# Rotary embedding applied head by head in the attention units, the first tile's blocks solved on VectorE, the third tile prepared with the first two

## What is computed

```python
qd, kd, vd = split(silu(short_conv(concat([qb, kb, vb]))))
qd, kd = l2_norm(qd per head), l2_norm(kd per head)
qd, kd = apply_rope(qd, cos, sin), apply_rope(kd, cos, sin)     # latent tokens only
# apply_rope, per pair: out = (x1*c - x2*s, x1*s + x2*c)
# per chunk: a = strict_lower((k*beta) @ k.T * decay); t_inv = inverse(eye + a)
# scan over chunks: v_new = t_inv-corrected values; o = q @ S + intra @ v_new; S = S*decay + k.T @ v_new
```

## Time and profile before

| | us |
|---|---|
| median of three runs | 1311.85 (1308.52 to 1314.66) |
| the profiled execution | 1310.18 |
| its span, first to last instruction | 1308.3 |
| attention units, about | 170 to 412 |
| delta phase: preparation | 412 to 473 |
| delta phase: loop over pairs | 473 to 634 |

### The profile page before, as it was taken

How to read it: one execution, slowest core, us unless ns; L and a number is a source line. 1 busy time by engine, 2 the same in 40 slices (tenths; PEclk the granted TensorE clock), 3 DMA queues, 4 the chain that set the end, 5 groups by cost and what they waited for, 6 DMA issues and landing times.

```text
span 1308.3 us, 15852 instructions
## 1 busy us (share of the span) xinstructions
PE 1148.9 (88%) x6262; PEld 615.6 (47%) x6262; DVE 435.0 (33%) x784; ACT 327.0 (25%) x585; POOL 194.8 (15%) x330
## 2 busy tenths in 40 slices
PE   2699999999989759589999999999839999999990
PEld 1244456666655458589544444444423333333330
DVE  1233036666655714355530200123341111111115
ACT  4021134544543323232321000011201111111111
POOL 0000020011000377474100000000110111111100
PEclk9799999999989869799999999999859999999995
DMA  7801241435110011310211111131615999999936
GB/s 319 353 16 58 96 167 67 162 112 193 65 65 31 19 25 24 101 23 5 93 69 60 65 64 65 65 145 80 241 39 181 393 380 369 385 384 385 382 126 245
DMA packets 44064, 199.98 MB, mean 153 GB/s; under 512 B 18321, under 2 KB 23905, under 8 KB 31953
## 3 DMA queue, kind: packets, MB, share of 16 engines
q1 hardware_dynamic: 28256, 142.03, 28.3%
q10 hardware_dynamic: 4608, 30.18, 6.2%
q0 software_dynamic: 11120, 26.70, 5.6%
HBM read 190.69 MB, written 22.87 MB: 163 GB/s over the span
## 4 chain that ended last, share of the span: by engine, by line
PE 78%; DMA 7%; DVE 5%; POOL 4%; issue 3%; ACT 2%; SPq 0%; POOLq 0%; DVEq 0%; ACTq 0%
PE bank L1599 24%; PE bank L2138 11%; PE bank L1704 9%; PE bank L2159 6%; DMA arena<-h_scratch,arena 3%; PE bank L1753 3%; PE bank L1995 3%; PE bank L1993 3%; PE bank L1690 2%; PE bank L2126 2%; PE bank L1856 2%; PE bank L1661 2%; PE bank L1557 2%; POOL arena L628 1%; DMA arena<-in_w_blocks 1%
## 5 line engine op out<-in xcount | busy, mean ns | idle before, releaser
L1599 PE MATMUL bank<-arena 128*128 128x512 f32 x720 | 316.0, 595 | 4.4 <-DVE arena L1094 3.5
L1599 PEld LDWEIGHTS bank<-arena 128*128 128x128 f32 x720 | 135.3, 190 | 169.5 <-issue 168.4
L2138 PE MATMUL bank<-arena 128*32 128x512 f32 x1536 | 172.9, 601 | 1.3 <-DVE arena L1512 1.3
L1704 PE MATMUL bank<-arena 128*128 128x320 f32 x384 | 121.9, 451 | 0.0
L2138 PEld LDWEIGHTS bank<-arena 128*32 128x32 f32 x1536 | 48.3, 110 | 108.4 <-issue 108.4
L2159 PE MATMUL bank<-arena 128*32 128x512 f32 x768 | 87.4, 595 | 0.8 <-ACT arena L1034 0.8
L1704 PEld LDWEIGHTS bank<-arena 128*128 128x128 f32 x384 | 68.5, 193 | 25.6 <-issue 2.0
L1525 DVE TENSOR_TENSOR arena<-arena,bank 128x256 f32<-128x256 f32 x24 | 10.1, 421 | 176.3 <-ACT arena L1028 176.3
L692 POOL DMA_INDIRECT y_scratch<-arena x24 | 24.4, 1015 | 248.2 <-DVE arena L1518 248.2
L1390 DVE TENSOR_TENSOR arena<-arena,bank 128x512 f32<-128x512 f32 x10 | 6.9, 687 | 135.8 <-PE bank L1995 135.8
L957 ACT ACTIVATE arena<-bank 128x512 f32<-128x512 f32 x20 | 11.9, 597 | 151.5 <-PE bank L1599 151.5
(11 more groups left out here) (292 smaller groups left out, 1522.8 us busy)
## 6 DMA issues: line engine op xcount, KB each, us to landing
arena<-in_w_up SPq DMA_DIRECT2D x32, 2048.0 KB, 15.4
arena<-in_w_blocks SPq DMA_DIRECT2D x27, 2048.0 KB
arena<-in_w_down ACTq DMA_DIRECT2D x28, 1024.0 KB, 8.9
arena<-y_scratch SPq DMA_DIRECT2D x10, 512.0 KB, 10.6
arena<-in_bias POOLq DMA_DIRECT2D x3, 1536.0 KB, 12.1
arena<-in_w_down SPq DMA_DIRECT2D x4, 1024.0 KB, 8.1
arena<-in_x SPq DMA_DIRECT2D x5, 512.0 KB, 9.6
gram_scratch<-arena SPq DMA_DIRECT2D x10, 256.0 KB, 2.5
```

The source lines that it names most:

```text
L1599: last = mm(bank, hT[:, k, tok0[i]:tok0[i] + P], w[:, k, :], start=(k == 0), stop=(k == KC - 1))
L1704: last = mm(banks[5 + half][:, 0:HTOK], w[:, k, :], hT[:, k, half * HTOK:(half + 1) * HTOK], start=(k == 0), stop=(k == KC - 1))
L2138: last = mm(banks[2 + e % 2][at, :], rowsT[e % 2][:, k, at], eup[expert % SLOTS_W][:, k, :], start=(k == 0), stop=(k == KC - 1))
```

## The change

- **Rotation.** The four rotated tiles of the preparation become `scaled(i)`: one instruction each. The rotation moves into the attention units, a head at a time for all four latent tiles (128 x 256 elements an instruction), in three parts of two instructions, in the units that are 11, 12 and 13 behind the chunk's start. Its sines and cosines are loaded by POOL during the attention (into the buffer of the context values), and ACT's square of the next head waits for the last part (`rope_done`), since the temporary shares the square's buffer.
- **First solve.** Pair 0's blocks are solved by DVE (`first_solve`: a copy, then 15 steps of a product and a negated sum along the row), in buffers of its own, and spread by DVE (`first_spread`). POOL makes the third mask of pair 0 at once and starts with pair 1's solve; its spread and solve of later pairs keep their form.
- **Third tile.** Pair 2's `row_sums`, `decay_exp`, `decay_pre`, `key_key`, `gram_out` and pair 1's `key_query`, `intra_out` are done in the preparation, so pass 0 of the loop has only its three levels. POOL solves pair 2 in pass 1, around the third mask.
- **SP.** The scratch traffic of pairs 0 to 2 stands ahead of the wait for the z gate, in a new order; `solved_out(0)` waits for DVE's `intra_out(1)`, which is behind `first_solve` on DVE.

The core of the diff:

```diff
@@ SP, in the queue ahead of gb0
-                if turn:
-                    sp.wait_ge(*read_by(IN_SLOT[slot][turn - 1]))
                 if name == "gb0":
                     gram_out(0)
                     blocks_in(0)
+                    gram_out(1)
+                    blocks_in(1)
                     solved_out(0)
-                    gram_out(1)
                     solved_back(0)
-                    for p in (1, 2):
-                        blocks_in(p)
-                        solved_out(p)
-                        solved_back(p)
-                        gram_out(p + 1)
+                    gram_out(2)
+                    solved_out(1)
+                    solved_back(1)
+                    blocks_in(2)
+                    solved_out(2)
+                    solved_back(2)
+                    gram_out(3)
+                if turn:
+                    sp.wait_ge(*read_by(IN_SLOT[slot][turn - 1]))
@@ POOL, attention
+                if m == 2:
+                    pool.wait_ge(S["pv_mm"], 8)
+                    pool.wait_ge(S["k_out"], 32)
+                    pool.dma_start(rope, t["rope"]...).then_inc(S["b_in"], 16)
@@ POOL, delta phase
             masks(0, 1)
             masks(0, 2)
-            solve(0, 0, SUB - 1)
-            spread_out(0)
+            masks(0, 3)
             for p in range(T):
                 if p == 0:
-                    solve(1, 0, 6)
-                    masks(0, 3)
-                    solve(1, 6, SUB - 1)
-                    q_scaled(1)
-                    masks(1, 1)
-                    pool.wait_ge(S["rope_done"], T)
-                    spread_out(1)
-                    masks(1, 2)
+                    solve(1, 0, SUB - 1)
+                elif p == 1:
+                    solve(2, 0, 6)
+                    masks(1, 3)
+                    solve(2, 6, SUB - 1)
                 else:
                     masks(p, 3)
-                    ...
+                if p + 1 < T:
+                    q_scaled(p + 1)
+                if 2 <= p < T - 1:
+                    solve(p + 1, 0, SUB - 1)
+                if p + 1 < T:
+                    masks(p + 1, 1)
+                    spread_out(p + 1)
+                    masks(p + 1, 2)
@@ ACT
             def head_squared(c):
                 act.wait_ge(S["tok_ready"], c + 1)
                 if c >= 1:
-                    act.wait_ge(S["sqsum"], c)
+                    act.wait_ge(S["rope_done"], c)
...
             kq_out(0)
             decay_exp(0)
+            kq_out(1)
+            kq_out(2)
             z_out(2)
-            kq_out(1)
+            decay_exp(1)
             z_out(3)
-            kq_out(2)
-            decay_exp(1)
-            z_out(4)
             kq_out(3)
             kq_out(4)
+            decay_exp(2)
+            z_out(4)
...
-                if p + 2 < T:
+                if 1 <= p < T - 2:
                     decay_exp(p + 2)
@@ DVE, attention
+            def rotated(c, part):
+                pairs = qkv[:, 1:T, c * P:(c + 1) * P].rearrange("p t (c two) -> p t c two", two=2)
+                x1, x2_ = pairs[:, :, :, 0], pairs[:, :, :, 1]
+                cos, sin = rope[:, :, 0, :], rope[:, :, 1, :]
+                if part == 0:
+                    dve.wait_ge(S["b_in"], 16)
+                    step(v.tensor_tensor(ropet[:, 0], x1, sin, ALU.mult))
+                    step(v.tensor_tensor(ropet[:, 1], x2_, sin, ALU.mult))
+                if part == 1:
+                    step(v.tensor_tensor(x1, x1, cos, ALU.mult))
+                    step(v.tensor_tensor(x2_, x2_, cos, ALU.mult))
+                if part == 2:
+                    step(v.tensor_tensor(x1, x1, ropet[:, 1], ALU.subtract))
+                    step(v.tensor_tensor(x2_, x2_, ropet[:, 0], ALU.add), "rope_done")
...
+                for part in range(3):
+                    if conv_chunk(u, 11 + part) is not None and conv_chunk(u, 11 + part) < 2 * H_B:
+                        rotated(conv_chunk(u, 11 + part), part)
@@ DVE, delta phase
+            def first_solve():
+                dve.wait_ge(S["first_io"], 32)
+                step(v.tensor_copy(first_g[0:32], first_raw[0:32].rearrange("p k i -> p i k")))
+                for i in range(1, SUB):
+                    part = first_t[0:64, 0:i * i].rearrange("p (c k) -> p c k", c=i)
+                    step(v.tensor_tensor(part, first_x[0:64, 0:i, 0:i], first_g[0:64, i, 0:i].unsqueeze(1).to_broadcast([64, i, i]), ALU.mult))
+                    step(v.tensor_reduce(first_x[0:64, 0:i, i:i + 1], part, AX_X, ALU.add, negate=True))
...
-            rotated(0)
+            scaled(0)
             decay_pre(0)
+            scaled(1)
             tok_out(11, 3, 2)
-            dve.wait_ge(S["b_in"], 32)
-            rotated(1)
+            scaled(4)
             gram_out(0)
-            rotated(4)
             intra_out(0)
+            x_flat = first_x[0:64].rearrange("p c i -> p (c i)")
+            step(v.memset(x_flat, 0.0))
+            step(v.memset(x_flat[:, 0:SUB * SUB:SUB + 1], 1.0))
             decay_pre(1)
-            rotated(2)
+            scaled(2)
+            scaled(3)
             gram_out(1)
-            rotated(3)
+            first_solve()
+            intra_out(1)
             dve.wait_ge(S["kqT_ready"], 2 * T)
-            dve.wait_ge(S["gexp_done"], 1)
+            decay_pre(2)
+            first_spread()
+            gram_out(2)
@@ PE, delta phase
             kq_turn(0)
             key_key(0)
-            z_block(2)
             kq_turn(1)
+            kq_turn(2)
+            z_mm(2, 0)
             key_query(0)
+            z_mm(2, 1)
+            row_sums(1)
             z_block(3)
-            kq_turn(2)
-            row_sums(1)
-            z_block(4)
             key_key(1)
             kq_turn(3)
             kq_turn(4)
             pe.wait_ge(S["kqT_ready"], 2 * T)
+            key_query(1)
+            z_mm(4, 0)
+            row_sums(2)
+            z_mm(4, 1)
+            key_key(2)
             turn_inv(0, 1)
```

More of the change, by code:

```diff
@@ L228, in build @@
         solve_t = ring[:, 0, solve_at + SUB * SUB:solve_at + 2 * SUB * SUB]
+        first = [unit[d]["xs"].rearrange("p h c -> p (h c)") for d in range(2)]
+        first_g, first_x, first_raw = (v.rearrange("p (a b) -> p a b", a=SUB) for v in
+                                       (first[0][:, 0:SUB * SUB], first[0][:, SUB * SUB:], first[1][:, 0:SUB * SUB]))
+        first_t = first[1][:, SUB * SUB:]
+        first_in = first_t[:, 0:2 * H_B * SUB].rearrange("p (u i) -> p u i", u=2 * H_B)
         solved_in = solve_t[:, 0:2 * H_B * SUB].rearrange("p (u i) -> p u i", u=2 * H_B)
@@ L414, in erow_of, with mask_of @@
             return unit[d]["erow"][(p - 1) % 3]
+        def mask_of(p, n, d):
+            return unit[d]["cstate"] if (p, n) == (0, 3) else unit[d]["mask"][(NL * p + n) % 2]
         def solve_at_io(p, k):
-            return 48 * p + {"blocks": 32, "solved": 48}[k]
+            return 48 * (p - 1) + {"blocks": 32, "solved": 48}[k]
         def step_at(p, k):
@@ L596, in masks @@
                     pool.wait_ge(S[f"prep{d}"], dprep_at(p, "gram"))
-                    if NL * p + n > 2:
+                    if p >= 1:
                         pool.wait_ge(S[f"x_mm{d}"], NL * p + n - 2)
-                    step(pool.tensor_tensor(U["mask"][(NL * p + n) % 2], U["gramT"][p % 2],
+                    step(pool.tensor_tensor(mask_of(p, n, d), U["gramT"][p % 2],
                                             level_mask[:, d, n - 1, :].unsqueeze(1).to_broadcast([P, H_B, P]), ALU.mult), f"msk{d}")
             def spread_out(p):
-                pool.wait_ge(S["solve_back"], 16 * (p + 1))
+                pool.wait_ge(S["solve_back"], 16 * p)
                 for d in range(2):
@@ L751, in _ @@
             act.wait_ge(S["kctxT_mm"], 1)
-            step(sc.activation(kctxT, banks[6][:, :].rearrange("p (a b) -> p a b", a=4), ACT.Copy), "kctxT_ready")
+            step(sc.activation(kctxT, banks[6][:, :].rearrange("p (a b) -> p a b", a=4), ACT.Copy))
             for u in range(2 * T):
@@ L825, in gate_decays @@
                 step(sc.activation(gt[:, 4:6, :], gt[:, 10:12, :], ACT.Exp))
-                step(sc.activation(gt[:, 9, :], gt[:, 9, :], ACT.Exp), "gexp_done")
+                step(sc.activation(gt[:, 9, :], gt[:, 9, :], ACT.Exp))
             def head_squared(c):
@@ L1838, in turn_inv @@
                     if n == 1:
[L1839 removed]
+                        if p:
+                            pe.wait_ge(S["spread"], 2 * p + d - 1)
+                        else:
+                            pe.wait_ge(S[f"prep{d}"], dprep_at(2, "gram"))
                         if d == 1:
@@ L1855, in couple @@
                     for h in range(H_B):
-                        last = mm(banks[2 * d][:, h * P:(h + 1) * P], U["mask"][(NL * p + n) % 2][:, h], U["inv"][:, h], start=True, stop=True)
```

(1 more changed line is left out.)

81 lines of the change are left out of this document (37 added, 44 removed).

## The result

The changed kernel takes 1290.68 us, median of four runs (1286.11 to 1291.0), against 1311.41 (1308.52 to 1314.66) of four runs of the kernel before: a ratio of 0.9833 with a 95% interval of 0.9806 to 0.986. That is 20.7 us faster, where 17.0 were forecast (1293, range 1286 to 1303).

What follows compares the result with a forecast made beforehand. PE bounds the attention units; in the delta phase PE waits, for SP's late send and POOL's late state store. Gains 9.0 + 9.4 + 2.1 = 20.5 less 3.5 give 17.0: 1310.2 to 1293 us, range 1286 to 1303.

Steps and rivals of the forecast that it cites:

- Part 1: Attention units: rotation adds 22.1 us of DVE work, mostly hidden; slips reaching PE at the conv turns cost 3.5 us.
- rival (d): Attention units: rotation parts reach PE and each brings a slow-clock stretch, 36 us lost, 1325.7 us; chance 0.04.
- Part 2: Preparation: earlier SP send and DVE's first solve bring the first turn of the inverse forward, 9.0 us gained.
- Rival (a): Preparation: `first_solve` no faster than POOL's solve or held up by it, 14.7 instead of 9.4, 1298.5 us; chance 0.10.
- Part 3: Pass 0: without `key_query(1)` and pair 2's decay chain it takes 17.5 instead of 26.9 us, 9.4 gained.
- Rival (e): Preparation: PE's own order holds pair 1 back, so it ends as late as before; 1302 us, chance 0.04.
- Part 4: Pass 1: POOL's waits are filled with solving, less its later start and ACT's table load; 2.1 us gained.
- The hole: End of pass 1: PE's wait before pass 2, ended by the state store, was to stay at 8 to 10 us.
- Rival (b): Pass 1: bound by POOL's chain with pair 2's whole solve inside, taking 44.3 us; 1299.5 us, chance 0.10.

Runs made afterwards that it cites:

- e3: Changed kernel with pair 0's blocks solved by POOL after its three masks instead of by DVE: 1285.25 us, ratio 0.981 to the kernel before.
- e1: Changed kernel without the rotation's 48 DVE instructions in the attention units (latent q and k stay unrotated): 1290.34 us, ratio 0.9839 to the kernel before.
- e4: Changed kernel with pair 2's row sums, decay, key products and gram back in pass 0: 1298.69 us, ratio 0.9916 to the kernel before.
- e5: Changed kernel with the context state store issued by ACT in pass 1 instead of by POOL: 1283.81 us, ratio 0.98 to the kernel before.
- e7: Kernel before with two edits only, SP's z gate wait behind the scratch traffic and the state store issued by ACT: 1286.28 us, ratio 0.9811.
- e2: Kernel before with one edit, SP's wait for the z gate put behind the scratch traffic of pairs 0 to 2: 1301.07 us, ratio 0.9923.

## Why the prediction was right

**Part 1, rotation: 3.5 forecast, 3.2 measured, but of another make.** The slip of the score by 0.92 is as forecast. Up to the turn near 374 PE lost 1.5 us (374.89 - 169.51 = 205.38 against 374.08 - 170.19 = 203.89), not 3.5: the slack at the turns takes more than I carried through. PE's waits at the turns grew by 0.4 in all (0.63 to 0.89 near 299, 1.90 to 2.04 near 374, the other three not at all). Two more, 0.25 each, are at the convolution (275.33 and 349.49, for ACT's copy `conv_in`), a place that the prediction hadn't named; the remaining 0.6 comes in small steps that no listed wait shows. The other 1.5 is the mechanism of rival (d) in small: behind the wait of 2.04 the turn already took 0.45 instead of 0.30, and the stretch up to 387.70 took 12.81 instead of 11.27. The granted clock in 370 to 400 is 0.83 against 0.89. The stretch takes 12.81 to 12.89 in the five kernels with the rotation and 11.26 to 11.31 in the five without. It happened once and not eight times. The forecast had no such term, so that 1.5 and 1.5 come near its 3.5 is partly luck.

**Part 2, preparation: 9.0 forecast, 10.25 measured.** The chain can be laid over the trace of after, less the 2.52 us by which the barrier is later: products 422.4 (422.4 measured), `row_sums(1)` 430.5 (430.6), table load 432.5 (432.7), decay done 439.0 (439.2), products of pair 1 443.0 (443.2), end of `first_solve` 452.0 (452.1). The first difference is behind it. I had added 0.5 for the meeting with POOL and 1 for the clock at `row_sums(2)`; the decay chain ended at 460.7, not at 461 to 462, since ACT goes on after the first eight matmuls, and the turn came at 462.9, not at 464.2.

`first_solve` itself took the 8.9 of the sum. The one product that met POOL's copy took 0.75 (row 451.25), its neighbours 0.28 and 0.33, so the meeting cost 0.45. The rule of the Trainium skill (SBUF — State Buffer, "SBUF: two separate sides"), that one of the two engines holds the port for a whole instruction, agrees with this row and with POOL's 0.33 beside DVE against 0.21 alone. Its price here was not the 2.4 worked out from it. Only the last four products ran beside POOL's solve, not eight, and at three of them POOL was the one that took longer (0.33, 0.41 and 0.44, alone 0.21, 0.24 and 0.27). Rival (a) is out; still, e3 shows that the comparison it made, DVE's solve against POOL's, was not the one that counts. It is where the solve stands: on DVE it is in front of `intra_out(1)`, which holds up PE; on POOL it would fill 19.54 us of idle time. I read the earlier trace rows for how slow POOL is, and not for when it is free.

**Part 3, pass 0: 9.4 forecast, 11.1 measured.** The term that was mis-sized is level 1. I took 7.0 from before, where PE came out of 13.38 us of idle time, and it took 5.3. The granted clock over this level was 0.66 before and 1.00 after, where PE had waited 2.96 and 1.02 only. That is how five of the six kernels with this pass 0 went (15.82 each); e1 took 17.44. I had the cause in hand in part 2, where the hole goes, and didn't carry it into part 3. Levels 2 and 3 took 5.3 and 5.2 as summed. e4 shows the rest of this part: pair 2's chain costs 10.1 in pass 0 and 4.8 in the preparation. Rival (e) is out: the preparation is 10.25 shorter than before, and 15.0 in e4.

**Part 4, pass 1: 2.1 forecast, 1.6 measured.** The hole stayed, 9.86, and is ended by the store as said (9.17 in front of ACT's table load). Rival (b) is out: POOL's gaps were filled. The term that was off is how much later POOL starts relative to PE, 3.4 (its masks end 1.36 ahead of the pass before, 1.99 behind its start after) where I took 2.9. The table load took 1.28 and the exponential started 1.29 after its start (511.29 and 512.58), as in the earlier trace rows; the 2.66 that the Trainium skill gives for a switch (ScalarE: Activation LUTs, "What ACT_TABLE_LOAD costs") is not seen here either. What the prediction didn't ask is who should issue the store: e5 and e7 price it at 7.9 and 12.0.

**The sum.** Stages: 10.25 + 11.1 + 1.6 + 0.4 (from pass 2 on) - 3.2 = 20.2 (forecast 17.0). The profiled executions differ by 24.1. Of the 3.9 left, 0.7 is ahead of the units, and 2.15 is one stretch of the router, far from the change: the same 16 matmuls at the lower clock before, at the upper after, behind the same wait of 3.63. Before, then after:

```profile
936.55 4.53 PE L2050 MATMUL bank<-arena 128*64 128x320 f32 x16 [3.63 <-ACT arena L741]
```

```profile
915.70 2.38 PE L2107 MATMUL bank<-arena 128*64 128x320 f32 x16 [3.63 <-ACT arena L759]
```

The medians differ by 20.7, close to the sum of the stages. Passes with the same code vary too: pass 2 takes 32.1 to 33.4 over the ten traces. So a stage difference is good to about 1.7 us, one such stretch, when it comes from one trace each. So it is partly luck that the forecast came within 2.3 us: it was 3.2 short in the stages and 7.1 in the profiled execution.

## What to carry to other kernels

Read first what stands in an in-order queue between a result and its user: here two waits, SP's for a weight slot and ACT's for a store issued behind POOL's work, were worth 24 us with two edits, against 21 for a change that holds the first of them and moves a rotation, a solve and a tile as well. When a serial step is given to a faster engine, look at what is queued behind it there and whether the slower one is idle then; 13.7 us on an idle POOL beat 8.9 on DVE. And count a hole twice when it goes: its length, and the slow matmuls behind it.

## What the hardware showed that was not expected

- The solve on DVE: products and sums of 1 to 225 columns took 0.14 to 0.39 us (but for the one of 0.75) with about 0.04 between dependent ones, so 31 instructions ran in 8.9 us. POOL's 15 steps (products of 15 to 64 columns, 0.21 to 0.33 us with 0.08 between) took 14.7 beside DVE's rotations, 13.2 in e2, 13.7 in e3.
- A large DVE product holds up a small POOL one: in e3 two POOL instructions of 0.26 and 0.27 took 1.13 and 1.19, beside two large DVE scalings (2.61 together).
- How long PE stays at the lower clock is not fixed by the wait before: behind 2.66 or 2.67 us the same eight matmuls took 6.69 in the trace of e1 and 5.07 to 5.37 in the nine others.
